# A block-wise triangular inverse whose first levels move to VectorE substitution, with norms packed in strips

## Chip, cores and metric

The kernel runs on one core of a Trainium2 chip. A time is the device time of one execution in microseconds (us), and lower is better. TensorE (PE in the rows; PEld are its weight loads), VectorE (DVE), ScalarE (ACT), GpSimd (POOL) and the DMA queue of SyncE (SP) each run their own instruction stream and meet only at semaphores.

## What is computed

One layer of a hybrid decoder trunk over 256 tokens of width 1024, all in float32: RMS norm with a conditioning vector, two parallel token mixers (causal pooling, and a gated delta rule over 8 heads of 128), a residual, and then a mixture of 32 experts of which each token takes 4. The part around the change is the delta rule. For each head and each chunk it solves a unit lower triangular system:

```python
q, k = l2norm(q) * dk**-0.5, l2norm(k)                 # per head of 128
kk = einsum('ik,jk->ij', k * beta[:, None], k) * decay
lhs = where(strict, kk, 0.0) + eye
rhs = concatenate([v * beta[:, None], k_beta * exp(g)[:, None]], axis=-1)
u, w = split(triangular_solve(lhs, rhs, lower=True))
v_new = u - w @ state
o = (q * exp(g)) @ state + (q @ k.T * decay) @ v_new
state = state * exp(g_last) + k_dec.T @ v_new
```

The output is the final RMS norm of the residual stream, 256 x 1024.

## The kernel before

**Weights.** All large weights pass through a ring of 6 slots of 2 MB. 30 chunks serve the mixers (numbers 21 `pool_out`, 22 and 23 `z`, 24 and 25 `gate1`, 26 and 27 `gdn_out`, 28 and 29 `w_out`; chunk n lies in slot n mod 6), then every expert takes 6 slots. SyncE's queue issues them strictly in that order, and each waits for `used[slot]`, which TensorE raises. In the mixers it is raised late: `free_slot(n)` puts a chunk on the list `done_chunk`, and the first matmul of the next call of `project` takes the last entry off the list (`carry`). The streams of experts 1 to 31 wait for `vec_route`, the result of the routing, and then for slots.

**Norms.** The squares of q and k (16 head tiles of 128 channels x 256 tokens) are summed over channels by 16 matmuls, each of which puts one head's sum into its own row of a 16-row result (L861). ScalarE takes the root, VectorE the reciprocal (L1397), and 16 matmuls with 16 contraction rows each spread a row over 128 partitions (L880), two per PSUM bank, which VectorE multiplies onto q and k (L1401). The first of four output pairs of the pooling branch (`pool_out_pair`) stands ahead of the spread, the other three behind it.

**Delta rule.** The 8 heads are done in two groups g of HG = 4, and the 256 tokens as two tiles t of 128. Each engine's program writes out the same order by hand, so a `matrices` tile is [128, 2 tiles, 4 heads, 128]. Per group: products k k and k q, the decay matrices, then L (`decay`) on VectorE (L1458, semaphore `vec_l`), two pairs of z projections on TensorE (`z_pair`, 16 matmuls of 256 columns each), the transposes of L, k and v (L964, L967, L969), their evacuation by VectorE (L1463, L1466 to L1470), and the inverse of I + L. The inverse starts with 2 by 2 blocks, `inv = I - off1 part` (L1475, L1477), and doubles the block in six levels s = 2, 4, 8, 16, 32, 64. A level is, for each t: GpSimd cuts out the off-diagonal part (L532), TensorE forms off x inv (L978), ScalarE copies the product to SBUF (L618), TensorE forms the two corrections (L985 for inv, L988 for its transpose), VectorE subtracts them (L1489, L1490). The last level has no L985. Then follow u and w (L994), the state and the outputs, and in the second group the four pairs of `gate1_pair` between them.

**After the mixers** come the z gating, two projections, the residual, the routing, and a loop over blocks of 64 tokens, 33 of them, each with the 12 MB of its expert's weights.

The functions as they stand:

Of the kernel before, what the change touches and what calls it, by code (L numbers as in the profile page):

```python
# [24 lines left out]
P = 128  # L25
# [7 lines left out]
LEVELS = (2, 4, 8, 16, 32, 64)  # L33
# [33 lines left out]
for _name, _w in (("ident", P), ("ones", P), ("causal", P), ("near", P), ("cross", P), ("strict", P), ("before", P),  # L67
                  ("off1", P), ("off1T", P), ("off2T", P), ("off4T", P), ("off8T", P), ("off16T", P),
                  ("off32T", P), ("off64T", P), ("iota", S + 1), ("row", 1),
                  ("pick", 2 * 2 * HEADS - 1), ("qscale", 1), ("count", len(WINDOWS) * 16), ("expert", E)):  # L70
    CONST[_name] = (_at, _w)
    _at += _w
# [3 lines left out]
def constants():  # L76
# [16 lines left out]
    for s in (1,) + LEVELS:  # L93
        off = (r // (2 * s) == q // (2 * s)) & (q // s % 2 == 1) & (r // s % 2 == 0)
        put(f"off{s}T", off)
        if s == 1:
            put("off1", off.T)
# [4 lines left out]
    put("pick", np.arange(2 * 2 * HEADS - 1) == 2 * HEADS - 1)  # L102
    put("qscale", np.where(np.arange(P) < HEADS, P, 1)[:, None])
# [5 lines left out]
def program(nc, x, c, ada_w, ada_b, norm_mix_g, norm_ffn_g, w_in, conv_w, pool_w, pool_scale, a_log,  # L109
            dt_bias, gdn_norm_g, w_pool_out, w_gdn_out, w_out, router_w, router_b, exp_w1, exp_b1,  # L110
            exp_w2, exp_b2, final_norm_g, const, out):
    with ExitStack() as ctx:
# [52 lines left out]
        norms = work[0:2 * HEADS, 0:S]  # L165
# [18 lines left out]
        lT, inv, invT, prod, off, eg_row, vb, kbg, kdec = (matrices(work, i) for i in range(9))  # L184
        state = work[:, 9216:9728].rearrange("p (h n) -> p h n", h=HG)
# [115 lines left out]
        vec_g = sem("vec_g")  # L301
        pe_g = sem("pe_g")
# [9 lines left out]
        vec_nat = sem("vec_nat")  # L312
# [3 lines left out]
        vec_inv = sem("vec_inv")  # L316
        pe_prod = sem("pe_prod")
# [178 lines left out]
        def _(pool):  # L496
# [14 lines left out]
            for g in range(2):  # L511
# [7 lines left out]
                for t in range(T):  # L519
                    b = 2 * g + t  # L520

                    pool.wait_ge(vec_l, b + 1)
                    nc.gpsimd.tensor_tensor(inv[:, t], decay[:, t], over_heads(const_tile("off1")),
                                            ALU.mult).then_inc(pool_off, 1)
                    pool.wait_ge(vec_lT, b + 1)
                    nc.gpsimd.tensor_tensor(invT[:, t], lT[:, t], over_heads(const_tile("off1T")),
                                            ALU.mult).then_inc(pool_off, 1)
                for i, s in enumerate(LEVELS):
                    for t in range(T):
                        if i:  # L530
                            pool.wait_ge(pe_prod, 12 * g + 2 * (i - 1) + t + 1)
# [13 lines left out]
        def _(act):  # L545
# [32 lines left out]
            for i in range(4):  # L578
                if i == 2:
# [8 lines left out]
            nc.scalar.activation(norms, bank[4][0:2 * HEADS, 0:S], ACT.Sqrt, scale=const_tile("qscale")[0:2 * HEADS, :],  # L588
                                 bias=small[0:2 * HEADS, 17:18]).then_inc(act_norm, 1)
# [12 lines left out]
            for g in range(2):  # L602
# [6 lines left out]
                z_copy(2 * g + 1)  # L609
                if g:  # L610
                    for i in range(2):
                        act.wait_ge(pe_gt1, i + 1)
                        nc.scalar.activation(gt1_row[:, i * 512:(i + 1) * 512], bank[6][:, :],
                                             ACT.Copy).then_inc(act_gt1, 1)
                for i in range(len(LEVELS)):
                    for t in range(T):
                        act.wait_ge(pe_prod, 12 * g + 2 * i + t + 1)
                        nc.scalar.activation(prod[:, t], quad(3 * t + 1), ACT.Copy).then_inc(act_prod, 1)  # L618
# [102 lines left out]
        def _(pe):  # L721
# [135 lines left out]
            for i in range(8):  # L857
                pe.wait_ge(pool_sq, i + 1)
                for a in range(2):
                    head = 2 * i + a  # L860
                    mm = nc.tensor.matmul(bank[4][0:2 * HEADS, 0:S],  # L861
                                          pick[:, 2 * HEADS - 1 - head:4 * HEADS - 1 - head],
# [854 lines left out]
```

## Time and profile before

| what | value |
| --- | --- |
| median of 3 runs | 1438.84 us (1435.74 to 1439.37) |
| the profiled execution, its own time | 1435.84 us |
| its span, first to last instruction | 1434.0 us, mean granted TensorE clock 0.979 |
| TensorE busy | 1326.1 us (92%) |
| VectorE, ScalarE, GpSimd busy | 404.7, 179.8, 73.5 us |
| chain that ended last | PE 53%, DMA 41%, DVE 3% |
| data moved | 471.79 MB, mean 329 GB/s |
| norms, from the sums of squares to the first product k k | 177.16 to 211.70 us |
| delta rule, group 0 and group 1 up to the end of the levels | 211.70 to 280.0, 290.96 to 357.75 us |
| loop over blocks | from about 475 us |

Times inside the execution count from the first instruction. A share of busy time is a mean over stages with different limits, so the stages are read one by one. Each float32 matmul leaves two records on PE.

### The profile page before, as it was taken

How to read it: one execution, taken by the hardware profiler on the slowest of the kernel's cores; microseconds unless marked ns; L12 is line 12 of the kernel's file. 1: busy time of each engine (PE TensorE's matmuls, PEld its weight loads, DVE VectorE, ACT ScalarE, POOL GpSimd, SP SyncE). 2: the span in 40 equal slices, each digit the busy share in tenths (PEclk: the TensorE clock that was granted, in tenths of full speed). 3: DMA queues.
4: the chain of work that ended last, by engine and by line, in shares of the span. 5: the costliest groups of instructions: out<-in, count | busy, mean ns of one | idle time of the engine just before them, and what ended most of it. 6: DMA issues, size and time to landing. Idle time of an engine off the chain costs nothing.

```text
span 1434.0 us, 17610 instructions
## 1 busy us (share of the span) xinstructions
PE 1326.1 (92%) x6633; PEld 656.6 (46%) x6634; DVE 404.7 (28%) x969; ACT 179.8 (13%) x366; POOL 73.5 (5%) x63
## 2 busy tenths in 40 slices
PE   4999998989999999999999989999999999999996
PEld 2888877868985333332233323333333333223332
DVE  1687435453224312111111112111111211111112
ACT  1000201221212101100010001100100110001002
POOL 1110004243100000000000000000000000000000
PEclk9999989999999899999999999999999999999998
DMA  9986631010344599999999999879999999999995
GB/s 375 375 324 235 237 116 59 1 59 1 121 154 176 227 425 426 428 427 425 425 427 427 427 424 425 368 318 428 426 428 424 425 428 428 425 425 428 427 426 210
DMA packets 65494, 471.79 MB, mean 329 GB/s; under 512 B 3981, under 2 KB 4298, under 8 KB 31546
## 3 DMA queue, kind: packets, MB, share of 16 engines
q1 hardware_dynamic: 64672, 469.78, 79.6%
q10 hardware_dynamic: 538, 1.13, 0.2%
q0 software_dynamic: 256, 0.48, 0.1%
q8 instruction: 20, 0.33, 0.1%
q14 instruction: 8, 0.07, 0.0%
HBM read 470.33 MB, written 1.05 MB: 329 GB/s over the span
## 4 chain that ended last, share of the span: by engine, by line
PE 53%; DMA 41%; DVE 3%; SPq 2%; issue 1%; ACT 1%; DVEq 0%
DMA ring<-in_exp_w_dram 39%; PE bank L1162 16%; PE bank L740 15%; PE bank L1188 5%; PE bank L1062 2%; PE bank L1133 2%; PE bank L988 2%; SPq L469 1%; PE bank L1200 1%; DMA ring<-in_w_in_dram 1%; PE bank L978 1%; PE bank L985 1%; PE bank L1154 1%; PE bank L880 1%; PE bank L861 0%
## 5 line engine op out<-in xcount | busy, mean ns | idle before, releaser
L1162 PE MATMUL bank<-ring,work 128*64 128x512 f32 x2112 | 472.8, 598 | 48.9 <-DMA ring<-in_exp_w_dram 48.9
L1162 PEld LDWEIGHTS bank<-ring,work 128*64 128x64 f32 x2112 | 145.1, 137 | 373.8 <-issue 274.3
L1188 PE MATMUL bank<-ring,work 128*64 128x512 f32 x1056 | 233.9, 595 | 0.0
L740 PE MATMUL bank<-region_h,ring 128*128 128x256 f32 x832 | 186.4, 385 | 4.6 <-DMA ring<-in_w_in_dram 3.1
L740 PEld LDWEIGHTS bank<-region_h,ring 128*128 128x128 f32 x832 | 159.0, 193 | 28.2 <-DMA ring<-in_w_in_dram 3.5
L1188 PEld LDWEIGHTS bank<-ring,work 128*64 128x64 f32 x1056 | 72.9, 137 | 137.4 <-issue 137.4
L1639 DVE TENSOR_SCALAR work<-bank 128x256 f32<-128x256 f32 x66 | 27.6, 418 | 348.1 <-PE bank L1162 348.1
L697 ACT ACTIVATE work<-work 128x256 f32<-128x256 f32 x66 | 27.5, 416 | 766.7 <-DVE work L1639 766.7
L1666 DVE TENSOR_TENSOR work<-bank,work 128x512 f32<-128x512 f32 x33 | 22.8, 692 | 315.7 <-PE bank L1188 315.7
L1133 PE MATMUL bank<-qkv,work 128*64 128x512 f32 x272 | 65.9, 606 | 0.6 <-DVE work L1579 0.6
L1200 PE MATMUL bank<-work 64*128 64x512 f32 x264 | 65.6, 615 | 0.8 <-DVE work L1666 0.8
L978 PE MATMUL bank<-work 128*128 128x128 f32 x192 | 30.0, 306 | 16.2 <-DVE work L1477 9.3
L1654 DVE TENSOR_SCALAR work<-consts,region_z 128x128 f32 (+1 forms) x66 | 19.9, 345 | 88.1 <-issue 88.1
L1646 DVE TENSOR_TENSOR work<-work 128x256 f32<-128x256 f32 x66 | 40.7, 617 | 12.3 <-DVE work L1642 12.3
L1200 PEld LDWEIGHTS bank<-work 64*128 64x128 f32 x264 | 22.7, 186 | 43.2 <-issue 41.5
L1133 PEld LDWEIGHTS bank<-qkv,work 128*64 128x64 f32 x272 | 19.8, 139 | 39.5 <-issue 39.5
L1154 PE MATMUL bank<-work 32*64 32x512 f32 x264 | 36.8, 627 | 0.7 <-issue 0.7
L1301 DVE SCALAR_TENSOR_TENSOR region_z<-ring,c_act,region_z 128x512 f32<-128x512 f32 x48 | 35.6, 808 | 0.0
L978 PEld LDWEIGHTS bank<-work 128*128 128x128 f32 x192 | 26.5, 214 | 18.8 <-POOL work L532 9.7
L532 POOL TENSOR_TENSOR work<-work,consts 128x512 f32<-128x512 f32 x24 | 32.2, 1343 | 35.4 <-PE bank L978 35.4
L1332 DVE SCALAR_TENSOR_TENSOR qkv<-bank,conv_cols,qkv 128x255 f32<-128x255 f32 (+2 forms) x72 | 31.4, 477 | 1.3
L740 PE MATMUL bank<-region_z,ring 128*128 128x256 f32 x128 | 27.9, 380 | 1.0 <-DVE region_z L1514 1.0
(280 smaller groups left out, 944.5 us busy)
## 6 DMA issues: line engine op xcount, KB each, us to landing
ring<-in_exp_w_dram SPq DMA_DIRECT2D x192, 2048.0 KB, 23.7
ring<-in_w_in_dram SPq DMA_DIRECT2D x13, 2048.0 KB, 13.5
ring<-in_ada_w_dram SPq DMA_DIRECT2D x12, 2048.0 KB, 13.8
ring<-in_w_gdn_out_dram SPq DMA_DIRECT2D x2, 2048.0 KB, 8.1
ring<-in_w_out_dram SPq DMA_DIRECT2D x2, 2048.0 KB, 7.8
ring<-in_w_pool_out_dram SPq DMA_DIRECT2D x1, 2048.0 KB, 8.1
consts<-in_const_dram SPq DMA_DIRECT2D x1, 1025.0 KB, 20.7
region_x<-in_x_dram SPq DMA_DIRECT2D x2, 512.0 KB, 4.4
```

Source lines behind the costliest of these rows:

```text
L532: nc.gpsimd.tensor_tensor(off[:, t], lT[:, t], over_heads(const_tile(f"off{s}T")), ALU.mult).then_inc(pool_off, 1)
L740: mm = nc.tensor.matmul(out_ap, w(k) if w else w_slot(n, j, k), rhs[:, k, :], start=(k == 0), stop=(k == kc - 1))
L978: mm = nc.tensor.matmul(quad(3 * t + 1)[:, h], off[:, t, h], inv[:, t, h], start=True, stop=True)
L988: mm = nc.tensor.matmul(quad(3 * t + 2)[:, h], prod[:, t, h], invT[:, t, h], start=True, stop=True)
L1133: mm = nc.tensor.matmul(bank[3][h * SLOTS:(h + 1) * SLOTS, :], sel[:, t, :], h2[:, t, h * 512:(h + 1) * 512], start=(t == 0), stop=(t == T ...
L1154: nc.tensor.matmul(bank[b][h * SLOTS:(h + 1) * SLOTS, :], onehot[b * SLOTS:b * SLOTS + E, :], b1_rows[b * SLOTS:b * SLOTS + E, h * 512:(h ...
L1162: mm = nc.tensor.matmul(bank[b][h * SLOTS:(h + 1) * SLOTS, :], xT[:, c % 4, c // 4, :], slot_as(q, 2)[:, i, lo:lo + 512], start=False, sto ...
L1188: mm = nc.tensor.matmul(bank[2][o * SLOTS:(o + 1) * SLOTS, :], actT[:, b, c, h, :], slot_as(4 + b, 2)[:, h, lo:lo + 512], start=(b + h + c ...
L1200: mm = nc.tensor.matmul(bank[4 + 2 * t + h][:, :], wselT[at, t * P:(t + 1) * P], y_nat[at, :], start=False, stop=last, skip_group_check=True)
L1301: ins = stt(half, w[:, k, :], c_act[:, k:k + 1], half, ALU.mult, ALU.add)
L1332: steps.append(stt(qkv[:, f, shift:S], src[:, a, 0:S - shift], w, qkv[:, f, shift:S], ALU.mult, ALU.add))
L1646: tt(act_nat[:, b, :].rearrange("q (c p) -> q p c", c=2), lin[:, b, :].rearrange("q (p c) -> q p c", c=2), sig[:, b, :].rearrange("q (p c) ...
```

## The change

The levels 2 and 4 of the inverse go away. In their place the 8 by 8 diagonal blocks are inverted directly: GpSimd masks L to its 8 by 8 blocks, VectorE squeezes them to 8 columns (a reduction over 16 blocks), spreads them to a [128, 256] tile per token tile, one TensorE matmul with a mask of 8 by 8 ones gives every row of a block the other rows' coefficients in PSUM, and VectorE runs 7 steps of two dependent instructions (multiply, subtract) for all heads and tiles at once, and spreads the result back. Level 32 forms the correction of `inv` in one quadrant only, level 64 forms all in one quadrant. The transposed inverse is made by transposing (4 transposes per tile, copied by ScalarE). v and k are scaled on the way out of PSUM by ScalarE in place of VectorE. Of the second z pair of each group one tile stands behind the new block matmul, the other is dealt out, two matmuls ahead of each level; its `Silu` copy moves behind the levels. The z matmuls no longer go through `project`. The norms use four 32-wide strips of the array: 4 rounds of 4 matmuls for the sums, and 4 rounds of 4 for the spread, each round followed by a pooling pair. The core of the diff:

```diff
-LEVELS = (2, 4, 8, 16, 32, 64)
+LEVELS = (8, 16, 32, 64)
+OCT = 8
...
# ScalarE
-                z_copy(2 * g + 1)
...
+                    for out_, b, what in ((kbg if t else kdec, 3 * t + 1, BEG if t else KDF), (vb, 3 * t + 2, BETA)):
+                        for h in range(HG):
+                            ins = nc.scalar.activation(out_[:, t, h], quad(b)[:, h], ACT.Copy,
+                                                       scale=heads_in[:, what, t, HG * g + h:HG * g + h + 1])
...
+                    act.wait_ge(pe_invT, 2 * g + t + 1)
+                    nc.scalar.activation(invT[:, t], quad(3 * t + 2), ACT.Copy).then_inc(act_invT, 1)
...
+                z_copy(2 * g + 1)
# TensorE
-                mm = nc.tensor.matmul(bank[4][0:2 * HEADS, 0:S],
-                                      pick[:, 2 * HEADS - 1 - head:4 * HEADS - 1 - head],
-                                      sq[:, i, a * S:(a + 1) * S], start=(head == 0), stop=(head == 2 * HEADS - 1))
+            for r in range(4):
+                pe.wait_ge(pool_sq, 2 * r + 2)
+                for j in range(4):
+                    mm = nc.tensor.matmul(bank[4][32 * j:32 * j + 32, 0:S], pick[:, 31 - r:63 - r],
+                                          sq[:, 2 * r + j // 2, (j % 2) * S:(j % 2 + 1) * S],
+                                          start=(r == 0), stop=(r == 3))
...
+            for r in range(4):
+                if r:
+                    pe.wait_ge(vec_norm, 4 * r)
+                for j in range(4):
+                    at = slice(32 * j, 32 * j + 32)
+                    mm = nc.tensor.matmul(bank[4 + j][:, 0:S],
+                                          ident[at, 32 * j + r:32 * j + r + 1].to_broadcast([32, P]), norms[at, :],
+                                          start=True, stop=True)
                 mm.then_inc(pe_norm, 1)
+                if r < 3:
+                    pool_out_pair(r + 1)
...
-                mm = project(pair(7)[:, a, :], n, 2 * (i % 2) + a, hT)
+                for k in range(lo, hi):
+                    mm = nc.tensor.matmul(pair(7)[:, a, :], w_slot(n, j, k), hT[:, k, :],
+                                          start=(k == 0), stop=(k == KC - 1))
...
+                pe.wait_ge(vec_oct, g + 1)
+                pe.wait_ge(vec_lT, 2 * g + 1)
+                nc.tensor.matmul(bank[0][:, :], const_tile("octs"), prod[:, 0].rearrange("p h n -> p (h n)"),
+                                 start=True, stop=True).then_inc(pe_oct, 1)
+                z_tile(2 * g + 1, 0)
...
+                for i, s in enumerate(LEVELS):
+                    z_tile(2 * g + 1, 1, 2 * i, 2 * i + 2)
...
+                                mm = nc.tensor.matmul(quad(3 * t + 1)[hi, h, lo], off[lo, t, h, hi], inv[lo, t, h, lo],
+                                                      start=True, stop=True)
# VectorE
+                link(copy(oct_all, lane.unsqueeze(1).to_broadcast([P, 2 * HG, OCT])))
+                for t in range(T):
+                    dve.wait_ge(pool_off, 10 * g + t + 1)
+                    link(nc.vector.tensor_reduce(oct_l[:, t], inv[:, t].rearrange("p h (b j) -> p h j b", j=OCT),
+                                                 AX.X, ALU.add))
+                    dve.wait_ge(pe_lT, 2 * g + t + 1)
+                    copy(lT[:, t], quad(3 * t)).then_inc(vec_lT, 1)
                 for t in range(T):
+                    ins = tt(oct_of[:, t], oct_l[:, t].unsqueeze(2).to_broadcast([P, HG, OCT, OCT]),
+                             lane.unsqueeze(1).unsqueeze(3).to_broadcast([P, HG, OCT, OCT]), ALU.mult)
+                ins.then_inc(vec_oct, 1)
+                dve.wait_ge(pe_oct, g + 1)
+                for k in range(OCT - 1, 0, -1):
+                    link(tt(oct_step[:, :, 0:k], oct_all[:, :, k:k + 1].to_broadcast([P, 2 * HG, k]),
+                            rows_of[:, :, k, 0:k], ALU.mult))
+                    link(tt(oct_all[:, :, 0:k], oct_all[:, :, 0:k], oct_step[:, :, 0:k], ALU.subtract))
+                for t in range(T):
+                    tt(inv[:, t].rearrange("p h (b j) -> p h b j", j=OCT),
+                       oct_inv[:, t].unsqueeze(2).to_broadcast([P, HG, P // OCT, OCT]),
+                       octs.unsqueeze(1).to_broadcast([P, HG, P // OCT, OCT]), ALU.mult).then_inc(vec_inv, 1)
```

`link` makes the next VectorE instruction wait for the semaphore of the one before.

## Rows read from the trace of the kernel before

**Rows 1.** Stages: length, PE, PEld, DVE, ACT, POOL busy (count), clock, DMA share, GB/s

```profile
187.82:197.75 9.93, 9.93 (x33) 7.05 (x33) 4.81 (x7) 0.00 (x0) 0.00 (x0) 0.75 0.44 166
197.75:210.93 13.18, 13.17 (x49) 10.86 (x48) 2.66 (x4) 0.00 (x0) 0.00 (x0) 0.80 0.00 0
211.70:242.18 30.48, 25.05 (x148) 21.19 (x149) 17.33 (x50) 4.78 (x7) 12.26 (x10) 0.97 0.20 70
242.18:280.00 37.82, 34.35 (x273) 33.20 (x273) 18.00 (x32) 7.17 (x12) 13.72 (x11) 0.93 0.00 1
...
319.27:357.75 38.48, 35.02 (x273) 33.86 (x273) 15.71 (x23) 7.16 (x12) 13.71 (x11) 0.92 0.00 1
```

**Rows 2.** Chain that ended last, in the block loop: start, us, what

```profile
504.97 13.88 PE bank L1162 x64
...
628.08 25.64 DMA ring<-in_exp_w_dram
```

**Rows 3.** Timeline of SyncE's queue (start, us, instruction), and one issue row

```profile
184.90 34.27 SPq L469 DMA_DIRECT2D ring<-in_w_gdn_out_dram  x2
...
482.89 26.20 SPq L477 DMA_DIRECT2D ring<-in_exp_w_dram  x7
ring<-in_w_gdn_out_dram SPq DMA_DIRECT2D x2, 2048.0 KB, 8.1
```

**Rows 4.** Timeline of the norms, PE and DVE

```profile
177.16 7.08 PE L861 MATMUL bank<-work,consts 128*16 128x256 f32 x32 [1.75 <-DVE work L1389]
184.87 1.74 DVE L1397 RECIPROCAL work<-work 16x256 f32<-16x256 f32 x1 [7.46 <-ACT work L588]
```

**Rows 5.** Matmuls in strips elsewhere, timeline and chain in order of time

```profile
17.58 1.92 PE L752 MATMUL bank<-ring,c_act 128*32 128x512 f32 x16
503.95 1.02 PE bank L1154 x8
```

**Rows 6.** Timeline from L to the first level

```profile
218.07 7.17 PE L740 MATMUL bank<-region_h,ring 128*128 128x256 f32 x32
225.32 1.12 DVE L1458 SCALAR_TENSOR_TENSOR region_x<-bank,heads_in,region_x 128x128 f32<-128x128 f32 x4
239.83 3.39 POOL L532 TENSOR_TENSOR work<-work,consts 128x512 f32<-128x512 f32 x2
240.34 1.74 DVE L1477 SCALAR_TENSOR_TENSOR work<-work,consts 128x512 f32<-128x512 f32 x1
242.18 2.05 PE L978 MATMUL bank<-work 128*128 128x128 f32 x8 [4.66 <-DVE work L1477]
244.31 1.27 POOL L532 TENSOR_TENSOR work<-work,consts 128x512 f32<-128x512 f32 x1 [1.10 <-PE bank L978]
301.39 1.12 DVE L1458 SCALAR_TENSOR_TENSOR region_x<-bank,heads_in,region_x 128x128 f32<-128x128 f32 x4
```

**Rows 7.** Timeline of one level at full clock

```profile
250.35 1.06 PE L978 MATMUL bank<-work 128*128 128x128 f32 x8
256.60 1.06 PE L978 MATMUL bank<-work 128*128 128x128 f32 x8
257.47 0.68 DVE L1490 TENSOR_TENSOR work<-work,bank 128x512 f32<-128x512 f32 x1
258.30 1.13 PE L978 MATMUL bank<-work 128*128 128x128 f32 x8 [0.65 <-DVE work L1490]
```

**Rows 8.** Timeline rows of small operations

```profile
160.63 1.43 DVE L1380 SCALAR_TENSOR_TENSOR heads_in<-heads_in 128x16 f32<-128x16 f32 x7
173.62 0.23 DVE L1386 COPY heads_in<-bank 128x64 f32<-128x64 f32 x1 [10.93 <-PE bank L843]
233.01 1.87 PE L950 MATMUL bank<-rw,mod 128*128 128x32 f32 x16
286.73 1.15 ACT L626 ACTIVATE qkv<-bank,heads_in 128x128 f32<-128x128 f32 x4 [3.19 <-PE bank L1017]
455.44 0.37 DVE L1554 TENSOR_REDUCE region_z<-region_z 128x32 f32<-128x128 f32 x1
```

More of the change, by code:

```diff
@@ L164, in program @@
         sq = work[:, 0:4096].rearrange("p (i n) -> p i n", i=8)
-        norms = work[0:2 * HEADS, 0:S]
+        norms = work[:, 0:S]
         u_pool = work[:, 4096:5120].rearrange("p (g s) -> p g s", g=4)
@@ L952, in _ @@
                     mm.then_inc(pe_rbias, 1)
[L953 to L958 removed]
                 for t in range(T):
[L960 removed]
                     tok = slice(t * P, (t + 1) * P)
[L962 removed]
+                    pe.wait_ge(vec_l, 2 * g + t + 1)
                     for h in hs:
@@ L970, in _ @@
                     mm.then_inc(pe_nat, 1)
-                for i in range(len(LEVELS)):
+                pe.wait_ge(vec_oct, g + 1)
[3 more added lines that the diff above has]
+                z_tile(2 * g + 1, 0)
+                if g:
+                    gt1_half(1)
+                for t in range(T):
+                    pe.wait_ge(vec_inv, 10 * g + t + 1)
+                    pe.wait_ge(act_nat2, 2 * g + t + 1)
+                    for h in range(HG):
+                        mm = nc.tensor.transpose(quad(3 * t + 2)[:, h], inv[:, t, h], ident)
+                    mm.then_inc(pe_invT, 1)
@@ L980, in _ @@
                         mm.then_inc(pe_prod, 1)
                     for t in range(T):
[L982 to L989 removed]
+                        pe.wait_ge(act_prod, 8 * g + 2 * i + t + 1)
@@ L1397, in _, with gate_pool @@
             recip(norms, norms).then_inc(vec_rnorm, 1)
-            for i in range(8):
-                dve.wait_ge(pe_norm, i + 1)
-                a = qkv[:, 2 * i:2 * i + 2, :]
-                tt(a, a, pair(4 + i % 2), ALU.mult).then_inc(vec_norm, 1)
-            for i in range(4):
+            def gate_pool(i):
                 dve.wait_ge(pe_pair, 18 + i + 1)
@@ L1407, in _ @@
                 tt(a, a, pair((18 + i) % 4), ALU.mult).then_inc(vec_pair, 1)
+            for r in range(4):
+                dve.wait_ge(pe_norm, r + 1)
+                for j in range(4):
+                    a = qkv[:, 4 * r + j, :]
+                    tt(a, a, bank[4 + j][:, 0:S], ALU.mult).then_inc(vec_norm, 1)
+                gate_pool(r)
             dve.wait_ge(act_ba, 3)
-            link(tt(heads_in[:, BEG], heads_in[:, BETA], heads_in[:, EG], ALU.mult))
+            tt(heads_in[:, BEG], heads_in[:, BETA], heads_in[:, EG], ALU.mult).then_inc(vec_beg, 1)
             def squares(b):
```

187 lines of the change are left out of this document (99 added, 88 removed).

## The prediction, as it stands on record

> **What bounds the kernel now.** I read four views: the chain that ended last in order of time, the busy time by stage, the DMA queue's timeline, and the timeline of the two stages that the diff touches.
>
> The chain says which parts matter for the end. In the block loop it alternates between TensorE for whole blocks and a transfer of 25.6 us per expert [rows 2]: the loop is bound by the arrival of expert weights, apart from stretches where the ring is full. This looks as if a shorter mixer stage could be worth nothing. The queue's timeline answers it: the stream of expert 1 is issued at 482.89 us [rows 3], after the routing, which itself comes after everything in the mixers. The queue isn't at work ahead of that on anything that the loop waits for: DMA share is 0.00 to 0.20 between 197 and 280 us [rows 1]. So the whole loop starts from the routing, and what the mixers lose or win moves the end one for one, until a mixer weight comes late.
>
> In the stages of the diff TensorE is almost always busy (34.35 of 37.82 us in the levels [rows 1]), yet it isn't at its work limit: it goes through a dependency loop of 6.25 us a level (256.60 - 250.35) [rows 7], and through narrow matmuls that use 16 of 128 columns or rows [rows 1, 4]. Three stretches also show a granted clock below 1: 0.75 and 0.80 at the norms, 0.93 and 0.92 in the levels, whose first products take 2.05 us against 1.06 us later [rows 1, 6, 7]. That is half clock, 1.2 GHz, and it comes after 4.66 us of idle TensorE.
>
> **Norms.** Before: 177.16 to 211.70 us, 34.5 us. Of it 7.08 us are the 16 summing matmuls [rows 4], 9.93 us the spreads, 13.18 us three pooling pairs [rows 1]. After:
> - Sums in four strips. Rows of the same form are the `ada` rows: 8 matmuls of 512 columns in 4 strips take 1.92 us [rows 5]. Sixteen of 256 columns hold as many, so 1.95 us. Bounds 1.9 and 7.08 (no overlap).
> - Pooling pair 0: half of the 7.17 us for 16 full matmuls [rows 6], 3.6 us. It covers the root and the 1.74 us reciprocal [rows 4], whose time goes by elements per partition, 256 in both kernels. Without that cover they would cost 2.6 us.
> - Four rounds of spread. Four matmuls with 32 contraction rows and 512 columns that run side by side take 1.02 us [rows 5]; with 256 columns about 0.6. Sum 2.4 us, bounds 2.0 and 7.1 (serial, 16 x 0.445). VectorE's 4 multiplications of a round lie beside the 3.6 us pooling pair.
> - Three pooling pairs at full clock: 10.7 us.
> - A new tail: behind the last round VectorE has 4 multiplications of 128x256 and one gate of 128x512 before `vec_pair` 6 lets the products start. A 128x128 one costs 1.12 / 4 = 0.28 us [rows 6], a 128x512 one 0.68 [rows 7], so 4 x 0.39 + 0.6 + 0.3 of semaphores = 2.5 us.
>
> 1.95 + 3.6 + 2.4 + 10.7 + 2.5 = 21.15 us against 34.5, a saving of 13.4 us. About 4 us of it is the clock returning to 2.4 GHz in this stage, which I expect since the long run of narrow matmuls ahead of its fall is gone; if it falls all the same, the saving is 9.5.
>
> The Trainium skill, page "TensorE: Matmul & The Clock Gate", section "Measured speedup vs the span model", gives 3.07 times for four row strips of 512 columns; by it the sums would take 7.08 / 3.07 = 2.3 us, an estimate that makes the whole saving 0.35 us smaller. The trace's own strips come out nearer 4 times (8 x 0.87 = 7 us of columns in 1.92), so I keep the row.
>
> **From L to the first level.** Before, from the end of L (226.44 us, 302.51 us) to the first L978: 15.7 and 16.8 us [rows 6, 1]. A pair of z projections lies in it. After, VectorE carries the path:
> - Identity copy 0.23; two reductions: a strided one of 128 elements takes 0.37 us [rows 8], 512 elements add 384 / 0.96 GHz = 0.4, so 0.8 each; two copies of the transposed L at 0.6: 3.0 us with the copy. In group 0 the transposes are 0.3 late, since 1.87 us of router products [rows 8] stand ahead of them.
> - Two spreads of 256 elements, 0.42 each. The second collides with GpSimd, which starts on `off8T` as the second transposed L lands. Two-operand SBUF work on both engines at once took 1.74 us on VectorE, where such a size takes 0.68 [rows 7], and 3.39 / 2 = 1.7 instead of 1.27 on GpSimd [rows 6]: +1.0. Together 1.85 us, bounds 0.8 and 2.9.
> - Block matmul, 512 columns: 1.0 us with semaphore.
> - Fourteen dependent instructions of 8 to 56 elements. The chain of 16-element ones goes at 1.43 / 7 = 0.205 us [rows 8], a copy of 64 from PSUM at 0.23 plus 0.04 for the link. Mean 0.235, sum 3.3 us, bounds 2.9 and 4.9 (0.35 each, should a PSUM operand or a broadcast cost more). TensorE's tile of 8 z matmuls (3.6 us) lies under it.
> - Spread back to `inv`, 0.65 + 0.6, then four transposes, 0.55.
>
> 3.0 + 1.85 + 1.0 + 3.3 + 1.25 + 0.55 = 10.95 us. Level 8 begins at 226.44 + 11.25 = 237.7 (before: 242.18) and 302.51 + 10.95 = 313.5 (before: 319.27).
>
> The Trainium skill, page "SBUF — State Buffer", section "SBUF: two separate sides", has the shared port pair of VectorE and GpSimd as a lock held for the whole instruction. By it the collision costs 1.27 us rather than 1.0. The row of 1.74 us lies close to either.
>
> The scaling of v and k moves to ScalarE: 16 instructions of 0.29 us [rows 8], 4.6 us, under VectorE's path and done some 3 us before `inv` needs the banks. Without that cover they would be the next thing late.
>
> **Levels.** Six cost 37.8 and 38.5 us [rows 1]. In each, TensorE waits 0.65 to 0.81 us for VectorE's last subtraction [rows 7]. After, two z matmuls (0.89 us) stand just there, so they cost 0.1: levels 8 and 16 take 6.3 each. Small products have unknown price: 8 matmuls of 32 columns took 1.87 us [rows 8], 0.23 each, as much as 128 columns, so the weight load sets it, but here the weights are also half as wide. Four take 0.45 to 0.9 us; middle 0.67. Level 32: 6.3 - 0.45 = 5.85. Level 64: 0.89 + 4 x 0.67 + 0.1 = 3.7. Sum 22.1 us (20.8 to 23.5).
>
> Ends: 237.7 + 22.1 = 259.8 against 280.0, saving 20.2; 313.5 + 22.1 = 335.6 against 357.75, saving 22.1. The first level's half clock (2 us of each saving) goes with the idle stretch that preceded it: the longest idle time left for TensorE is about 2 us, behind the transposes.
>
> **What is moved.** The second z pair no longer frees slots through `project`. `pool_out`'s slot 3 was freed by the first z pair, and the second `gdn_out` chunk issued there, at 184.90 + 34.27 = 219.2 us [rows 3]. Now 21, 22 and 23 lie on the list until `gate1_pair`, which takes them last in, first out; slot 3 comes free at its second pair, and three chunks queue there. At 8.1 us to land [rows 3], even one after the other, they are in after 24 us. From there to the use of the first lie five pairs of full projections, at 7.17 us [rows 6] 36 us, and two more to the output weights, 50 us. So this costs nothing; without that cover it would be up to 24 us. The late z copy on ScalarE lies beside gate products: nothing.
>
> **Sum.** 13.4 + 20.2 + 22.1 = 55.7 us. The profiled execution took 1435.84 us, so 1380.1. It lies 3.0 under the median of the runs shown; between the two bases I say 1382.
>
> **Rivals.**
> - *The substitution and its feeders are dearer, or the clock stays low in places.* At 0.35 us a step (+1.6 a group), serial strips (+9.8), full-price quadrants (+1.3 a group), and a clock that falls once a group and at the norms (+8 in all) the saving is 32. The time is 1382 + 24 = 1406. For it: only bounds exist for three of these prices. Against: the strip rows. Chance 0.14 for a saving of 30 to 44.
> - *Better than summed.* No collision, 0.2 us a step, quadrants at half price: -4.5 a group, a saving of 65: 1373. Chance 0.06 for more than 63.
> - *No gain: the end hangs on transfers that don't move.* If the expert stream were the bound from the start, the time would stay 1436 to 1439. Against: it is issued after the routing [rows 3]. Chance 0.02.
> - *Slower: the clock.* It falls at the narrow strips and stays at half through the levels. Each full-clock microsecond of TensorE in this stage costs one more at 1.2 GHz. Norms to levels hold about 115 us of such work in the new kernel; if it ran at 1.2 GHz throughout, the loss would be 115 against a saving of 56, 1497. It decides from 56 us of half-clock work. For it: 0.75 and 0.80 in the narrow stage [rows 1]. Against: full clock in most of the levels. Chance 0.03.
>
> **Numbers.** The forecast (saving 44 to 63 us, 1374 to 1393) has 0.75. The range 1372 to 1395 holds 0.8 (savings of 43 to 65). A change within 0.3% (4.3 us) can't be told from none. Faster: 0.75 + 0.14 + 0.06 = 0.95; same 0.02; slower 0.03.
>
> **What the profile after would show.** Sums in about 2 us and products k k near 198 us; first level near 224 and the levels in about 22 us each; no clock below 1 in them; fourteen short instructions in 3.3 us; a first L978 within 0.2 us of the z matmuls ahead of it; the expert stream 56 us earlier, and from there the same loop. Wrong would be: strips one after the other, short instructions near 0.4 us, TensorE idle over 3 us before the transposes, or a chain through a `gdn_out` or `w_out` transfer.

## The result, and the profile after

The changed kernel takes 1385.97 us (median of 4 runs, 1383.09 to 1390.67) against 1438.16 us for the kernel before in the same comparison. The ratio is 0.9646, 95% interval 0.9633 to 0.9659, so it is 52 us faster. The forecast was 1382 with a range of 1372 to 1395. The profiled execution took 1386.72 us, its span 1384.9 us with a mean granted clock of 0.984.

Both profiles are cut at the same events: the first sum of squares, the first product k k, the first transpose of L, the first product of a level (L978 before, L1025 after), and the first product of u. All numbers are differences of start times on PE.

| stretch, us | before | after | saved |
| --- | --- | --- | --- |
| first instruction to first sum | 177.16 | 179.71 | -2.55 |
| norms, to first k k | 34.54 | 21.25 | 13.29 |
| group 0: k k to transposes | 23.01 | 16.69 | 6.32 |
| group 0: transposes to first level | 7.47 | 12.19 | -4.72 |
| group 0: levels | 37.72 | 21.11 | 16.61 |
| group 0: u to group 1's k k | 7.74 | 7.69 | 0.05 |
| group 1: k k to transposes | 24.18 | 14.40 | 9.78 |
| group 1: transposes to first level | 7.45 | 14.71 | -7.26 |
| group 1: levels | 38.38 | 21.41 | 16.97 |
| from there to the end | 1076.35 | 1075.74 | 0.61 |

The middle eight rows save 51.0 us, and the rest of the program passes that on: the stream of expert 1 is issued at 433.64 us against 482.89 [rows 3], and from there to the end it takes 951.3 us against 951.1. The loop still alternates between whole blocks and transfers of 25.6 us, as in [rows 2]. The first line of the table isn't the change's: over all profiled executions of this study, whose programs do the same work up to there, it lies between 176.5 and 181.2 us. The last line varies too, between 1072.5 and 1078.1 us, so single executions differ by some us that no edit made.

The busy time by stage, columns as in [rows 1], of the changed kernel:

```profile
179.71:185.23 5.52, 5.52 (x49) 3.90 (x49) 1.97 (x3) 2.08 (x3) 0.00 (x0) 1.00 1.05 390
185.23:200.96 15.73, 13.60 (x82) 10.12 (x81) 8.11 (x22) 0.00 (x0) 0.00 (x0) 1.00 0.48 177
200.96:208.94 7.98, 7.98 (x45) 6.31 (x45) 4.95 (x19) 0.38 (x1) 0.00 (x0) 0.79 0.00 0
208.94:228.98 20.04, 17.20 (x101) 14.71 (x99) 15.98 (x50) 8.45 (x23) 10.17 (x8) 1.00 0.01 2
228.98:250.95 21.97, 21.86 (x194) 20.52 (x192) 8.30 (x18) 5.14 (x10) 7.50 (x6) 1.00 0.01 1
...
265.10:286.88 21.78, 18.59 (x100) 15.88 (x99) 15.42 (x45) 9.36 (x25) 10.18 (x8) 0.92 0.00 0
286.88:309.16 22.28, 22.04 (x194) 20.54 (x192) 7.57 (x13) 5.25 (x10) 7.53 (x6) 1.00 0.01 2
```

The levels answer to the last two kinds of line in [rows 1]: 37.8 and 38.5 us have become 22.0 and 22.3 with TensorE busy nearly throughout. The clock column (the granted TensorE clock as a share of 2.4 GHz) has moved its dips: none in the norms or the levels, but 0.79 at the first products and 0.92 between L and the levels of group 1.

The timeline of the changed kernel, norms:

```profile
179.71 1.93 PE L891 MATMUL bank<-work,consts 128*32 128x256 f32 x32 [1.75 <-DVE work L1446]
185.23 0.71 PE L910 MATMUL bank<-work,consts 32*128 32x256 f32 x8
198.89 1.41 DVE L1465 TENSOR_TENSOR qkv<-qkv,bank 128x256 f32<-128x256 f32 x4 [2.28 <-PE bank L910]
200.96 2.07 PE L969 MATMUL bank<-qkv 128*128 128x128 f32 x8 [2.13 <-DVE region_y L1459]
```

The sums take 1.93 us where they took 7.08 [rows 4]. The last line shows the new tail: TensorE waits 2.13 us for VectorE, and then its products run at half clock, 2.07 us for eight records that take 1.06 at full clock [rows 7].

From L to the first level, both groups:

```profile
217.44 1.12 DVE L1525 TENSOR_REDUCE work<-work 128x32 f32<-128x512 f32 x1
220.94 1.82 DVE L1530 TENSOR_TENSOR work<-work,consts 128x256 f32<-128x256 f32 x2
222.82 1.12 PE L1007 MATMUL bank<-work,consts 128*128 128x512 f32 x2 [2.35 <-DVE work L1530]
223.98 0.21 DVE L1536 TENSOR_TENSOR work<-work,bank 128x56 f32<-128x56 f32 x1 [1.22 <-PE bank L1007]
226.93 0.17 DVE L1538 TENSOR_TENSOR work<-work 128x8 f32<-128x8 f32 x1
227.14 1.29 DVE L1540 TENSOR_TENSOR work<-work,consts 128x512 f32<-128x512 f32 x2
...
279.01 1.68 PE L1007 MATMUL bank<-work,consts 128*128 128x512 f32 x2 [3.19 <-DVE work L1530]
280.49 4.79 PE L926 MATMUL bank<-region_h,ring 128*128 128x256 f32 x16
```

The fourteen dependent instructions run from 223.98 to 227.10 us. In group 1 the block product takes 1.68 us instead of 1.12 and the z tile 4.79 instead of 3.62. The clock in short stretches shows why (columns as above):

```profile
276.00:279.00 3.00, 0.00 (x0) 0.00 (x0) 2.92 (x4) 2.88 (x12) 2.23 (x2) 1.00 0.00 0
279.00:280.00 1.00, 0.99 (x2) 0.63 (x3) 0.00 (x0) 0.00 (x0) 0.00 (x0) 0.72 0.00 0
280.00:282.00 2.00, 2.00 (x5) 1.23 (x4) 1.10 (x6) 0.00 (x0) 0.00 (x0) 0.50 0.00 0
282.00:284.00 2.00, 2.00 (x8) 1.68 (x8) 1.69 (x10) 0.00 (x0) 0.00 (x0) 0.79 0.00 0
```

TensorE is idle for 3.19 us at a granted clock of 1.00, and half clock (1.2 GHz) follows after work has begun again.

### The profile page after: what moved, and what is told of

It is laid out like the page before. It is cut to its first block, busy times and chain, and to the rows that moved or that the text cites. A ratio compares the mean times of both kernels' runs of the same rounds, so it can differ in the third digit from the quotient of the medians.

```text
span 1384.9 us, 17303 instructions
## 1 busy us (share of the span) xinstructions
PE 1288.4 (93%) x6461; PEld 621.9 (45%) x6462; DVE 392.9 (28%) x987; ACT 184.7 (13%) x394; POOL 56.9 (4%) x51
## 4 chain that ended last, share of the span: by engine, by line
PE 51%; DMA 42%; DVE 3%; SPq 2%; issue 1%; ACT 1%; POOL 0%; DVEq 0%
DMA ring<-in_exp_w_dram 41%; PE bank L1219 17%; PE bank L771 13%; PE bank L1245 6%; PE bank L1119 2%; PE bank L1190 2%; DMA ring<-in_w_in_dram 2%; PE bank L1257 1%; SPq L481 1%; PE bank L1211 1%; PE bank L926 1%; PE bank L1041 1%; PE bank L1025 1%; PE bank L1038 1%; PE bank L816 0%
## 5 line engine op out<-in xcount | busy, mean ns | idle before, releaser
L771 PEld LDWEIGHTS bank<-region_h,ring 128*128 128x128 f32 x704 | 135.3, 194 | 21.3 <-DMA ring<-in_w_in_dram 2.8
L1713 DVE SCALAR_TENSOR_TENSOR work<-work 128x256 f32<-128x256 f32 x66 | 28.1, 425 | 2.3
L1119 PE MATMUL bank<-ring,region_y 128*128 128x512 f32 x64 | 28.2, 594 | 0.0
## 6 DMA issues: line engine op xcount, KB each, us to landing
ring<-in_w_out_dram SPq DMA_DIRECT2D x2, 2048.0 KB, 15.3
```

The source lines that it names most:

```text
L771: mm = nc.tensor.matmul(out_ap, w(k) if w else w_slot(n, j, k), rhs[:, k, :], start=(k == 0), stop=(k == kc - 1))
L1119: mm = nc.tensor.matmul(bank[4 + n][:, :], region_y[:, k, t * P:(t + 1) * P], ring[:, chunk_no["w_out"][h] % RING, k, :], start=(k == 0), ...
L1713: stt(lin[:, b, :], lin[:, b, :], 1.0, glu[:, b, :], ALU.add, ALU.mult).then_inc(vec_lin, 1)
```

## Experiments

Every experiment is an edit of the changed kernel. "Stage" is the time from the first sum to the first product of u in group 1, 129.45 us in the changed kernel and 180.49 before, taken from one profiled execution each. It leaves out the start and the end, which vary. The half clock lies at other places in each execution, and the text says where it touches a comparison. The medians and ratios are against the kernel before on the same chip.

| run | stage | mean clock in it | median | ratio, 95% interval |
| --- | --- | --- | --- | --- |
| changed kernel | 129.45 | 0.97 | 1385.97 | 0.9646 (0.9633 to 0.9659) |
| e1 norms as before | 139.79 | 0.95 | 1393.66 | 0.9705 (0.9687 to 0.9722) |
| e2 z in front | 144.71 | 0.94 | 1402.87 | 0.9762 (0.9747 to 0.9777) |
| e3 full products | 133.70 | 0.96 | 1387.79 | 0.9659 (0.9646 to 0.9672) |
| e4 scaling on VectorE | 132.55 | 0.96 | 1388.39 | 0.9664 (0.965 to 0.9677) |
| e5 gap filled with z work | 132.38 | 0.95 | 1387.05 | 0.9646 (0.9633 to 0.9659) |
| e6 copies on ScalarE | 126.02 | 0.99 | 1381.85 | 0.9616 (0.9603 to 0.9629) |
| e7 split last pair | 128.60 | 0.96 | 1384.43 | 0.963 (0.9615 to 0.9644) |
| e8 blocks of 4 | 135.99 | 0.97 | 1392.23 | 0.9685 (0.967 to 0.97) |
| e9 TensorE kept at work | 126.13 | 1.00 | 1383.27 | 0.9618 (0.9605 to 0.9631) |
| e10 e6 and e7 together | 123.23 | 1.00 | 1378.63 | 0.9595 (0.9582 to 0.9608) |
| e11 e10 and e9's idea | 123.24 | 1.00 | 1379.31 | 0.9595 (0.9582 to 0.9608) |
| e12 contiguous reduction | 126.27 | 0.99 | 1380.3, one run | |

### e1: the norms as before

```diff
-                for j in range(4):
-                    mm = nc.tensor.matmul(bank[4][32 * j:32 * j + 32, 0:S], pick[:, 31 - r:63 - r],
+                for a in range(2):
+                    head = 2 * i + a
+                    mm = nc.tensor.matmul(bank[4][0:2 * HEADS, 0:S],
+                                          pick[:, 2 * HEADS - 1 - head:4 * HEADS - 1 - head],
...
-                if r < 3:
-                    pool_out_pair(r + 1)
+            for i in range(1, 4):
+                pool_out_pair(i)
```

> The changed kernel with the norms as they were (one row per head, 16 narrow sums, 16 narrow spreads, no interleaving). Theory of the ledger: the strips give 13.3 us up to the first product, and 1.6 of that is lost again because TensorE is idle for 2.1 us ahead of the first product and falls to half clock there; so this kernel is 11 to 12 us slower than the changed one (about 1398), needs 34 to 35 us from the first sum to the first product, and the first product runs at full clock. Rival (the strips matter little, the stage was held by the clock alone): if the clock stays up in this run, the stage is only 4 us longer than in the changed kernel.

The norms took 34.40 us and the first products ran at full clock, as expected: 13.15 us more for the norms, against 1.6 us less at the products. The whole stage is 10.3 us longer: this execution kept full clock ahead of the levels of group 1, where the changed kernel's profile hadn't (1.7 us), and had half clock there in group 0 (0.8 us). The medians differ by 7.7 us, less than the expected 11 to 12, and the intervals of the ratios lie clear of each other.

The rival spoke of a kernel whose clock stays up in the norms, and here it didn't. The timeline, and a stretch inside the spreads, columns as in [rows 1]:

```profile
188.29 11.00 PE L911 MATMUL bank<-work,consts 16*128 16x256 f32 x32
199.22 12.03 PE L771 MATMUL bank<-work,ring 128*128 128x256 f32 x48
```

```profile
194.00:196.00 2.00, 2.00 (x6) 1.62 (x5) 0.77 (x2) 0.00 (x0) 0.00 (x0) 0.50 0.00 0
```

TensorE is busy throughout, and yet the clock falls to 0.50 at about 192 us, within the narrow spreads, and stays there until about 202 us. The kernel before has the same between 193 and 203 us; the changed kernel has 1.00 throughout its norms. As an estimate, the 16 spreads at full clock take as long as the 16 sums of as many columns, 7.1 us, and three pooling pairs take 3 x 3.65 us, as in the changed kernel. By it about 5 of the 13.15 us are half clock and about 8 are the packing. So the rival's 4 us at full clock look too few, but no run here has the old norms at full clock.

### e2: both z pairs in front

```diff
-                z_tile(2 * g, 0)
-                z_tile(2 * g, 1)
+                for i in (2 * g, 2 * g + 1):
+                    z_tile(i, 0)
+                    z_tile(i, 1)
...
-                    z_tile(2 * g + 1, 1, 2 * i, 2 * i + 2)
```

> The changed kernel with both z pairs of a group ahead of the transposes, as before, nothing dealt out. Theory: the z work stood under VectorE's substitution and in the gaps of the levels for nothing, so in front it costs 7.2 + 0.8 us a group, less 1.3 (the first reduction is done meanwhile) and less about 1 (the levels lose four fillers of 0.89 and get their gaps of 0.65 back): +5.5 us a group, +11 in all, and TensorE is then idle for over 5 us during the substitution, after which the first level runs at half clock, +2 a group: +13 to +16 us, about 1400. Rival (the dealing out is worth nothing, since TensorE's work is what counts): the same time as the changed kernel, 1386.

The stage is 15.3 us longer, the time 17 us, just above the expected 13 to 16. The timeline of this kernel in group 0 shows the idle stretch that the z tile had filled, and the half clock behind it (1.97 us for eight transposes' records that take 1.04, and 2.80 for sixteen that take 1.95):

```profile
233.99 1.97 PE L1016 MATMUL bank<-consts,work 128*128 128x128 f32 x8 [3.94 <-DVE work L1539]
235.75 2.80 PE L1024 MATMUL bank<-work 128*128 128x128 f32 x16
```

So dealing out the z work is worth as much as any part of the change that was taken back here: without it the substitution's time on VectorE lies open on TensorE.

### e3: full products in levels 32 and 64

```diff
-                            if s < HALF:
...
-                            else:
-                                mm = nc.tensor.matmul(quad(3 * t + 1)[hi, h, lo], off[lo, t, h, hi], inv[lo, t, h, lo],
-                                                      start=True, stop=True)
```

> The changed kernel with the products of levels 32 and 64 in full size. Theory: from the changed kernel's rows level 32 takes 6.06 us against 6.28 in full, level 64 3.35 against about 4.6, so +1.5 us a group, +3 in all: 1389. Rival (the weight load sets the price of small products, as with 32 columns): under +0.8 in all.

The levels take 22.59 and 22.91 us against 21.11 and 21.41: +1.48 and +1.50, the expected size. (The other 1.3 us of the longer stage are half clock in group 1.) The medians differ by 1.8 us, which the overlapping intervals don't separate. Eight quadrant products take 1.14 us in the changed kernel:

```profile
248.56 1.14 PE L1028 MATMUL bank<-work 64*64 64x64 f32 x16
```

Four cost 0.57 us, against 0.89 in full size. Half the columns alone would give 0.45, so the price lies between that and the full one.

### e4: v and k scaled by VectorE

```diff
+                    tt(vb[:, t], quad(3 * t + 2), heads(BETA, t), ALU.mult)
+                    if t:
+                        ins = tt(kbg[:, t], quad(3 * t + 1), heads(BEG, t), ALU.mult)
...
-                            ins = nc.scalar.activation(out_[:, t, h], quad(b)[:, h], ACT.Copy,
-                                                       scale=heads_in[:, what, t, HG * g + h:HG * g + h + 1])
```

> The changed kernel with v and k scaled by VectorE again, right behind its copies of the transposed L. Theory: VectorE carries the path to the first level, so its four instructions of 0.6 us cost 2.4 us a group, +4.8 in all, less about 1 because the collision of the second spread with GpSimd goes away: +3 to +5, about 1390; and with TensorE idle for over 4.5 us ahead of the block product the clock falls in both groups. Rival (TensorE's z tile is the longer arm): no change.

The stretch to the first level grows from 12.19 to 14.31 and from 14.71 to 16.02 us, +3.4 in all, at the low end of what was expected. In medians it is +2.4 us, which the overlapping intervals don't separate. TensorE was idle for 3.65 and 4.50 us ahead of the block product, and half clock followed in both groups, as expected. From the transposes to the block product it is 1.3 us more in each group (6.46 us against 5.17, 7.28 against 5.97): VectorE sets that part, and this is its price. The other 0.8 us, in group 0, are half clock behind it, where TensorE's z tile was then the longer arm (the inverse's transposes waited for nothing).

This kernel also settles the collision with GpSimd, which has finished its cut before the spreads start:

```profile
223.50 0.75 DVE L1531 TENSOR_TENSOR work<-work,consts 128x256 f32<-128x256 f32 x2
```

The two spreads take 0.75 us against 1.82 in the changed kernel, so the collision costs 1.07 us there. It is why four instructions of 0.6 us cost 1.3 and not 2.4.

### e5: the idle stretch filled with z work that was to be done anyway

```diff
+                if g:
+                    gt1_half(1)
+                z_tile(2 * g + 1, 0, 0, 4)
                 pe.wait_ge(vec_oct, g + 1)
...
-                z_tile(2 * g + 1, 0)
-                if g:
-                    gt1_half(1)
+                z_tile(2 * g + 1, 0, 4, 8)
```

> The changed kernel with half of the z tile (4 matmuls), and in the second group the residual-gate spread, moved from behind the block product to ahead of it, into the 2.4 and 3.2 us for which TensorE is idle there. Theory: in the profiled run the idle 3.2 us of the second group are followed by half clock for 3 us, which makes the block product 0.56 us and the z tile 1.2 us longer; with the gap filled the clock stays at 2.4 GHz and the level starts when VectorE is ready, saving 1.5 to 2.5 us in the second group and about 0.3 in the first: 1383 to 1384. Rival (the fall is an accident of where the gap lies and comes back elsewhere): within 0.5 us of the changed kernel, with a clock below 1 behind the block product instead.

No gain: the ratio is that of the changed kernel. The theory as put there fell, and its rival held. (Of the 2.9 us by which the stage is longer, 1.6 lie at the first products, ahead of the edit.) The timeline and clock of this kernel in group 0:

```profile
226.80 1.89 PE L926 MATMUL bank<-region_h,ring 128*128 128x256 f32 x8
230.91 1.90 PE L1017 MATMUL bank<-consts,work 128*128 128x128 f32 x8 [2.22 <-DVE work L1541]
```

```profile
228.00:231.00 3.00, 0.78 (x5) 0.35 (x4) 2.66 (x12) 0.00 (x0) 0.00 (x0) 1.00 0.00 0
231.00:234.00 3.00, 3.00 (x12) 2.73 (x13) 1.73 (x10) 1.20 (x2) 0.00 (x0) 0.51 0.00 0
```

The z tile had covered the substitution. Half of it moved away leaves 2.2 us idle behind the block product, and the half clock follows there. There is one amount of cover and two gaps.

### e6: the transposed L copied by ScalarE

```diff
-                    dve.wait_ge(pe_lT, 2 * g + t + 1)
-                    copy(lT[:, t], quad(3 * t)).then_inc(vec_lT, 1)
...
+                    act.wait_ge(pe_lT, 2 * g + t + 1)
+                    nc.scalar.activation(lT[:, t], quad(3 * t), ACT.Copy).then_inc(vec_lT, 1)
```

> The changed kernel with the two copies of the transposed L made by ScalarE in place of VectorE. Theory: VectorE carries the path, the copies cost it 1.2 us plus 0.1 of waits a group, and GpSimd's cut for level 8 starts earlier and no longer meets the spreads (another 0.5 to 1): -1.3 to -2.3 us a group in the first, less in the second where TensorE's own order (z tile, then the spread) binds: -2.5 to -4 in all, 1382 to 1383.5. Rival (the longer arm is TensorE): 0 in the second group, -0.5 in the first.

The stretch to the first level is 11.39 us in group 0 (12.19) and 13.63 in group 1 (14.71), and 11.40 and 12.02 in e10, where no half clock disturbs it. Against 12.20 and 13.00 in e9 that is -0.8 and -1.0 us from the edit, less than the expected 2.5 to 4 in all: the two spreads still meet GpSimd (2.04 and 1.83 us), so that part of the theory fell. The stage is 3.4 us shorter and the median 4 us, inside or near the expected numbers only because 1.6 us of the stage is the clock at the first products, which stayed up here although the gap was the same 2.14 us. So a gap of 2 us is followed by half clock in some executions and not in others.

### e7: the last pooling pair split around the last round

```diff
-                if r < 3:
+                if r < 2:
                     pool_out_pair(r + 1)
+                else:
+                    pool_out_half(3, r - 2)
```

> The changed kernel with the last round of norms between the two halves of the last pooling pair, so that VectorE multiplies while TensorE computes. Theory: the idle 2.1 us ahead of the first product shrink to about 1.0 us and the clock doesn't fall there (1.6 us): -1.1 to -2.7 us, 1383.5 to 1385. Rival (the clock falls there whatever the gap, after the stage of narrow matmuls): -1.1 us alone, with 0.5 still granted in the first products.

The norms take 20.09 us (-1.16), the gap is 0.78 us instead of 2.13, and the first products run at full clock: 15.08 us to the transposes against 16.69. The profiled execution had half clock in the two later gaps instead and so shows only -0.85 in all; in e10 and e11 the 1.16 us stand as they are. The median is 1.5 us lower, which the overlapping intervals don't separate.

### e8: 4 by 4 blocks, level 4 by products

```diff
-LEVELS = (8, 16, 32, 64)
-OCT = 8
+LEVELS = (4, 8, 16, 32, 64)
+OCT = 4
```

> The changed kernel with 4 by 4 blocks by substitution and level 4 by products: 6 dependent instructions in place of 14, a block product of 128 columns in place of 512, one level more. Theory: the level costs 6.3 us; the substitution saves 1.9 on VectorE and the block product and the spreads about 1.2, but TensorE's z tile of 3.6 us lies over it and is then the longer arm, so only 1.1 to 2 come back: +4 to +5 us a group, +8 to +10 in all, 1395. Rival (VectorE alone sets this stretch): +3 a group, 1392.

The levels grow by 6.07 and 5.77 us, the stretch ahead of them shrinks by 3.0 and 3.8: +6.5 us in the stage, +6.3 in medians. That is nearer the rival: VectorE's shorter path counts almost in full in group 0, since the z tile starts earlier too. In group 1 it is 2.1 us against the 13.00 of e9, which has no half clock there. Eight by eight is the better size by 3.0 us in group 0 and 3.6 in group 1.

### e9: TensorE kept at work in the gaps

```diff
+            pe.wait_ge(vec_pair, 3)
+            for k in range(4):
+                nc.tensor.matmul(pair(2)[:, 0, :], wp[:, k, 0:P], y_pool[:, k, :], start=(k == 0), stop=(k == 3))
...
+                for k in range(4):
+                    nc.tensor.matmul(pair(7)[:, 0, :], hT[:, k, 0:P], hT[:, k, :], start=(k == 0), stop=(k == 3))
                 pe.wait_ge(vec_oct, g + 1)
```

> The changed kernel with idle TensorE kept at work: 4 matmuls of 256 columns whose result is overwritten stand in the 2.1 us gap ahead of the first product, and 4 such in the 2.4 and 3.2 us gaps ahead of the block product, 1.8 us each. Nothing else is touched. Theory (idle gaps of 2 to 3 us are what the clock falls behind): 2.4 GHz from the first sum to the end of the levels, so the stage to the transposes takes 15.1 us and not 16.7 to 18.3, and the stretch from the transposes to the first level 12.2 in group 0 and 13.0 in group 1: -3.3 us against the profiled run of the changed kernel, time about 1383. Rival (the fall hangs on the narrow and small products, not on the gap): the half clock stays, no change.

The whole stage in one line each, the changed kernel, then this one:

```profile
179.71:309.16 129.45, 120.78 (x860) 103.97 (x860) 71.08 (x191) 35.10 (x77) 35.38 (x28) 0.97 0.11 39
```

```profile
178.62:304.75 126.13, 122.86 (x884) 105.64 (x884) 71.04 (x191) 35.09 (x77) 35.36 (x28) 1.00 0.11 40
```

More work on TensorE (122.86 us busy against 120.78), no half clock, and 3.3 us less time: 15.09 and 14.40 us to the transposes, 12.20 and 13.00 us to the first level, the sizes expected to within 0.1. The median is 2.7 us lower; the interval of the ratio, 0.9605 to 0.9631, lies just clear of 0.9633 to 0.9659. The rival falls, since narrow and small products are all still there.

One execution without half clock could be chance, so count the idle stretches of TensorE in this stage over the profiles of the changed kernel and all edits but e2, where two lie close together. Of 16 that last 2.1 to 2.4 us, 11 are followed by half clock and 5 aren't. Of four that last 3.1 to 3.2 us, three are. Of five that last 1.4 to 1.8 us, none is.

### e10 and e11: the parts together

> The changed kernel with ScalarE's copies of the transposed L and with the split last pooling pair. Theory: the parts add: 20.1 us for the norms (-1.15), 11.4 and 13.0 us from the transposes to the first level (-0.8 and about -1.3 against runs at full clock). From the first sum to the end of the levels 122.5 to 125 us against 129.45: time 1380 to 1382. Rival: the clock falls in other places for it and takes 2 to 3 us back.

> The kernel of the run before with TensorE kept at work in what is left of the gaps: 2 overwritten matmuls ahead of the first product, 3 ahead of the block product. If gaps set the clock: 122.5 us from the first sum to the end of the levels, no half clock there, 1379 to 1381, the fastest of all. If they don't: as the run before, or up to 0.5 us slower.

e10 is e6 and e7 in one kernel. Its stage:

```profile
180.15:303.38 123.23, 117.71 (x860) 101.33 (x860) 68.96 (x187) 37.15 (x81) 35.17 (x28) 1.00 0.11 41
```

It takes 1378.63 us, ratio 0.9595 (0.9582 to 0.9608), clear of the changed kernel and of e7; the interval of e6 overlaps it a little. The parts add, as the theory had it, and the time is below the 1380 to 1382 that were expected. The overwritten matmuls of e11 add nothing to it (123.24 us, the same ratio), since this profile has no half clock left to remove. That isn't assured in every execution. The block product of group 1 has the same gap ahead of it in e6 and in e10, and half clock behind it in e6 alone:

```profile
272.42 2.08 PE L1010 MATMUL bank<-work,consts 128*128 128x512 f32 x2 [2.18 <-DVE work L1531]
```

```profile
274.88 1.13 PE L1020 MATMUL bank<-work,consts 128*128 128x512 f32 x2 [2.19 <-DVE work L1541]
```

### e12: the reduction over neighbours

```diff
-                    link(nc.vector.tensor_reduce(oct_l[:, t], inv[:, t].rearrange("p h (b j) -> p h j b", j=OCT),
+                    link(nc.vector.tensor_reduce(oct_l[:, t], inv[:, t].rearrange("p h (j b) -> p h j b", j=OCT),
```

> The changed kernel, but the squeeze of the masked L adds 16 neighbouring elements in place of 16 that lie 8 apart, so what it computes in the block inverse is not the reference's; count and size of all instructions are the same. Theory (the stride doubles the price): each reduction takes 0.62 us, as other contiguous ones of 512 elements do, in place of 1.10 to 1.12, and the stretch to the first level is 0.9 us shorter a group. Rival (the price is that of a small inner extent of 16, or of GpSimd working beside it): 1.1 us again.

```profile
216.08 0.69 DVE L1525 TENSOR_REDUCE work<-work 128x32 f32<-128x512 f32 x1
```

0.69 us against 1.12 for the same 512 elements in 32 sums, with GpSimd at work beside it as before, so the 0.43 us are the stride. The stretch is 0.63 us shorter in group 0, not 0.9, because VectorE then waits for the transposes. Group 1 is 2.55 us shorter, 1.7 of which is the clock.

## Why the prediction was right, point by point

**The loop passes the mixers' gain on.** Right: 951.3 against 951.1 us from the first stream of expert 1 to the end.

**Norms, 21.15 us.** Measured 21.25: sums 1.93 (1.95), rounds 0.64 apart (0.6), 2.85 us from the last round to the first product, 2.2 without the round's own 0.64 (forecast 2.5). The three pooling pairs took 10.95 (10.7) and the one ahead of the spreads 3.65 (3.6), so the terms' errors cancel in part. About 5 of the 13.3 us saved are the clock (forecast about 4): the kernel before spent 9.93 and 13.18 us where full clock takes 7.1 and 10.95. The overlap is 7.08 / 1.93 = 3.7 times, above the 3.07 that the Trainium skill, page "TensorE: Matmul & The Clock Gate", section "Measured speedup vs the span model", gives for four row strips. These sums are strips of another kind, 32 output columns at the full 128 contraction rows, so the page's figure isn't for them; the row of the same form was the better guide.

**L to the first level.** The terms, as measured in group 0:
- Reductions: 1.12 and 1.10 us, not 0.8. This term was mis-sized by 0.6 us a group, of which group 0 pays half, as the forecast had allowed 0.3 there for late transposes. The one strided row that it was scaled from had 128 elements, and I added the rest at the contiguous rate; e12 shows that the stride costs 0.43 us in 512 elements. The Trainium skill, page "SBUF — State Buffer", section "Door 1: The DMA port swizzle", has a line of 16 bytes, and a penalty for each access that crosses to a new one; a stride of 8 floats does so each time. The measurement agrees in kind.
- Spreads with the collision: 1.82 us, as forecast (1.85). The collision itself is 1.07 us by e4, nearer the forecast's 1.0 than the 1.27 that it gave beside it.
- From the spreads to the first of the fourteen instructions 1.22 us (1.0), the fourteen 3.12 us (3.3), spread back 1.29 (1.25).
- Level 8 began 11.67 us after the end of L in group 0 (228.98 - 217.31; forecast 11.25), and 13.35 in group 1 (286.88 - 273.53; forecast 10.95). Of the 2.4 us in group 1, 1.7 are half clock. The rest is mostly the reductions. In group 1 TensorE also has the residual-gate spread (0.89 us) between its z tile and the inverse's transposes, which the forecast left out of this path. The transposes wait for no other engine there, even at full clock in e9, so TensorE's arm has become as long as VectorE's.

**The half clock.** This is the step that failed. The forecast's sign, "no clock below 1 in them", was about the levels, and there it holds. But it tied half clock to the 4.66 us idle stretch that the change removes, expected the longest idle time left to be "about 2 us", and put what follows the new gaps at nothing. The gaps are 2.13, 2.35 and 3.19 us; the last, before the inverse's transposes, is over the 3 us that it had named as a sign of being wrong. The profiled execution has half clock behind two of them, 1.6 us at the first products and 1.7 us in group 1. e9 shows the cause: with the gaps filled and all else equal, those 3.3 us are gone. e5 shows that moving work from one gap to another does not do it. What decides whether a gap of 2 us is followed by half clock stays open.

**Levels, 22.1 us.** Measured 21.97 and 22.28 with the first z filler. Level 32 took more than forecast (6.06 against 5.85) and level 64 less (3.35 against 3.7). The two errors cancel in part. The z matmuls ahead of each level cost next to nothing, as forecast: levels 8 and 16 of group 0 take 6.28 us each against 6.25 before.

**Scaling on ScalarE, late slots.** The scaling ran 219.28 to 223.53 us, over 4 us ahead of its need. The second `gdn_out` chunk was issued at 323.4 us instead of 219.2; from the levels' end to the expert stream it takes 124.48 us against 125.24, so nothing waited for it.

**Sum.** Forecast 55.7 us. In the stage it was 51.0; with the half clock of e9 taken off it is 54.4. From there the reductions account for about 0.9 of the 1.3 us by the rows above; no run takes their price off alone at full clock in the whole stage. The gain in medians is 52.2. The stage fell 4.7 us short and the time came out 4 us above 1382; what lies between the two is within the variation of the start and the end. 3.3 of the 4.7 us are the half clock behind the gaps.

## What to carry to other kernels

Work that moves to another engine is cheap only as long as the first engine has something independent to do meanwhile: here the dealt-out z matmuls are worth 15 us of stage time, more than the 10 us of the packed norms. When a change shortens an idle stretch of TensorE, look at the gaps that it leaves or makes, not only at the one it removes, and try to split a neighbouring block of real work around them. For a strided operand take the price from a row with the same stride and length, not from a short one.

## What the runs showed of the hardware that was not expected

- Half clock after gaps of only 2.1 to 3.2 us, in some executions and not in others: 16.69 us from the first products to the transposes in the changed kernel, 15.09 in e6 with the same gap of 2.14 us. Behind the gaps of 1.4 to 1.8 us in these profiles there is none.
- Where it falls varies: e5 and e8, whose code up to there is the changed kernel's, need 18.25 us for that same stretch.
- Half clock without a gap: it begins within a run of narrow matmuls (16 contraction rows) that keep TensorE busy, in the kernel before and in e1, and lasts about 10 us, full-size matmuls included.
- Two 128x256 spreads on VectorE, with both operands in SBUF: 1.82 us when GpSimd works beside them, 0.75 when it doesn't (e4).
- A reduction with a stride of 8 elements on VectorE: 1.10 to 1.12 us for 512 elements against 0.69 for neighbours (e12).
- 64x64 products with 64x64 weights: 0.57 us for four, against 0.89 for four of 128x128 (changed kernel, e3).
